# Adding the gated expert sums to the residual rows with accumulating DMAs instead of VectorE

## The reference, cut to what matters

```python
# routed_experts: y_assign holds each row's two expert outputs, wts their weights
y = einsum('tkd,tk->td', y_assign.reshape(T, 2, D), wts)
# run_trunk, after the experts
x = x + g2 * y                       # g2: a per-channel gate, one for the prompt, one for the sample
return rms_norm(x, norm_final)       # x * rsqrt(mean(x*x) + 1e-6) * norm_final
```

## Time and profile before

| What | Value |
|---|---|
| median of three runs | 1786.58 us |
| span of the profiled execution, first to last instruction | 1783.6 us |
| median less that span | 3.0 us |
| VectorE busy over the whole span | 71% |
| TensorE busy over the whole span | 91% |
| last expert matmul | 1726 us |
| first tail matmul | 1741.16 us |
| last VectorE instruction ends | 1778.8 us |

### The profile page before, as it was taken

One profiled execution on the slowest core, in us unless ns is written; L12 is line 12 of the kernel. 1 busy time (PEld: TensorE's weight loads), 2 busy tenths in 40 slices (PEclk: granted clock), 3 DMA queues, 4 the chain that ended last, 5 costly groups with the idle time before them and its releaser, 6 DMA issues. The chain is left out here.

```text
span 1783.6 us, 26138 instructions
## 1 busy us (share of the span) xinstructions
PE 1620.1 (91%) x10760; PEld 1416.7 (79%) x10760; DVE 1268.5 (71%) x1509; ACT 935.0 (52%) x1138; POOL 294.1 (16%) x187
## 2 busy tenths in 40 slices
PE   3679999999989999999798998499999999999956
PEld 2459988998889999999698786388888888888842
DVE  2535266627767768585765536799999999999947
ACT  2624233623443636353201211488888989898932
POOL 0110000200110102010200000124443232323130
PEclk9789999999999999999899998699999999999987
DMA  9822101210120202113343533699999999999966
GB/s 349 326 51 61 50 25 37 95 44 25 37 90 25 88 27 63 40 51 124 122 150 136 183 126 140 246 348 380 385 387 391 390 380 387 377 389 389 383 217 242
DMA packets 129219, 345.98 MB, mean 194 GB/s; under 512 B 16034, under 2 KB 71946, under 8 KB 103436
## 3 DMA queue, kind: packets, MB, share of 16 engines
q1 hardware_dynamic: 113180, 312.37, 48.1%
q0 software_dynamic: 9824, 17.88, 2.7%
q10 hardware_dynamic: 6096, 14.04, 2.1%
HBM read 316.15 MB, written 43.83 MB: 202 GB/s over the span
## 5 line engine op out<-in xcount | busy, mean ns | idle before, releaser
L140 PE MATMUL x_psum_proj<-h_hi,x_w_hi 128*128 128x364 f32 (+1 forms) x1120 | 381.1, 340 | 9.3 <-ACT x_x L796 6.1
L141 PE MATMUL x_psum_proj<-h_lo,x_w_hi 128*128 128x364 f32 (+1 forms) x1120 | 369.8, 330 | 0.0
L142 PE MATMUL x_psum_proj<-h_hi,x_w_lo 128*128 128x364 f32 (+1 forms) x1120 | 369.4, 330 | 0.0
L140 PEld LDWEIGHTS x_psum_proj<-h_hi,x_w_hi 128*128 128x128 f32 x1120 | 211.9, 189 | 17.6 <-ACT x_x L796 7.3
L141 PEld LDWEIGHTS x_psum_proj<-h_lo,x_w_hi 128*128 128x128 f32 x1120 | 212.1, 189 | 2.4
L142 PEld LDWEIGHTS x_psum_proj<-h_hi,x_w_lo 128*128 128x128 f32 x1120 | 212.0, 189 | 0.0
L572 POOL CAST x_w_hi<-x_w 128x1024 fp32r<-128x1024 f32 x44 | 73.5, 1671 | 636.4 <-PE x_psum_proj L142 633.8
L1978 POOL DMA_INDIRECT scratch_y<-e_y,all_tbl x32 | 73.6, 2300 | 374.9 <-ACT e_y L2091 362.1
L1186 DVE TENSOR_REDUCE x_sc<-x_diag 64x64 f32<-64x448 f32 x136 | 126.6, 931 | 1.1
L1211 DVE TENSOR_TENSOR x_w_lo<-x_w,x_w_hi 128x1024 fp32r<-128x1024 f32 x52 | 64.3, 1237 | 72.5 <-POOL x_w_hi L572 72.3
L140 PE MATMUL e_psum_g<-e_g_hi,e_x_hi 128*128 128x512 f32 x256 | 104.9, 410 | 9.6 <-DVE e_x_lo L2215 9.6
(11 more groups left out here) (350 smaller groups left out, 3775.0 us busy)
## 6 DMA issues: line engine op xcount, KB each, us to landing
mg_ring_hi<-in_w_e_gate SPq DMA_DIRECT2D x34, 1024.0 KB, 9.7
mg_ring_lo<-in_w_e_down SPq DMA_DIRECT2D x34, 1024.0 KB, 8.5
mg_ring_hi<-in_w_e_up SPq DMA_DIRECT2D x32, 1024.0 KB, 8.2
mg_ring_lo<-in_w_e_up SPq DMA_DIRECT2D x32, 1024.0 KB, 8.2
mg_ring_lo<-in_w_e_gate SPq DMA_DIRECT2D x30, 1024.0 KB, 9.3
mg_ring_hi<-in_w_e_down SPq DMA_DIRECT2D x30, 1024.0 KB, 7.9
c_w<-in_w_ada SPq DMA_DIRECT2D x12, 2048.0 KB, 15.0
x_w<-in_w_in SPq DMA_DIRECT2D x44, 512.0 KB, 3.9
```

Of the source, the lines that this page charges most:

```text
L140: nc.tensor.matmul(out, lhs[0], rhs[0], start=start, stop=False)
L141: nc.tensor.matmul(out, lhs[0], rhs[1], start=False, stop=False)
L142: return nc.tensor.matmul(out, lhs[1], rhs[0], start=False, stop=stop)
```

## The change

`x3_ready` becomes nine semaphores, one per tile. VectorE's `mixed(t)` ends with the gated product in `ys[t, 1]`. GpSimd, once it has raised `combined` and seen that the residual rows are loaded, waits for each `y_gated` in turn and issues one DMA from chip memory to chip memory that adds `ys[t, 1]` to `x3[t]`. ScalarE's `square(t)` waits for that DMA's semaphore.

```diff
+        x3_ready = [s.sem(f"x3_ready{t}") for t in range(NTT)]
...
             pool.sem_inc(combined, 1)
+            pool.wait_ge(x2_in, 16 * 3)
+            for t in range(NTT):
+                n = TILES[t][1]
+                pool.wait_ge(y_gated, t + 1)
+                pool.dma_start(x3[t][0:n], ys[0:n, t, 1, :], accum_op=ALU.add).then_inc(x3_ready[t], 16)
...
             def square(t):
                 n = TILES[t][1]
-                act.wait_ge(x3_ready, t + 1)
+                act.wait_ge(x3_ready[t], 16)
...
                     V.tensor_tensor(yt, sums[t % 2][0:n, :], g2[0:n, g, :], ALU.mult).then_inc(y_gated, 1)
-                dve.wait_ge(y_gated, t + 1)
-                V.tensor_tensor(x3[t][0:n], x3[t][0:n], yt, ALU.add).then_inc(x3_ready, 1)
-
             def normed(i):
```

More of the change, by code:

```diff
@@ L1904, in experts @@
         rows_in, x2_in, y_in = s.sem("rows_in"), s.sem("x2_in"), [s.sem(f"y_in{t}") for t in range(NTT)]
-        y_scaled, y_summed, y_gated, x3_ready, sumsq, rstd_act, rstd_dve, out_ready, out_done = (
-            s.sem("y_scaled"), s.sem("y_summed"), s.sem("y_gated"), s.sem("x3_ready"), s.sem("sumsq"), s.sem("rstd_act"),
+        x3_ready = [s.sem(f"x3_ready{t}") for t in range(NTT)]
+        y_scaled, y_summed, y_gated, sumsq, rstd_act, rstd_dve, out_ready, out_done = (
+            s.sem("y_scaled"), s.sem("y_summed"), s.sem("y_gated"), s.sem("sumsq"), s.sem("rstd_act"),
             s.sem("rstd_dve"), s.sem("out_ready"), s.sem("out_done"))
```

## The result

| | before | changed |
|---|---|---|
| median, runs of one chip | 1786.89 us (4 runs, 1786.47 to 1787.41) | 1801.74 us (4 runs, 1800.95 to 1803.04) |
| ratio, 95% interval | | 1.0088 (1.0075 to 1.0101) |
| span of the profiled execution | 1783.6 us | 1801.2 us |

The change makes the kernel slower by 14.9 us by the medians; the forecast was 1801.5. The profiled execution of the changed kernel took 1803.04 us, so 1.84 lie outside its span (the 3.0 of the prediction compared two different executions). To compare tails I measure in every profile from ScalarE's first instruction of the tail (1736.14 before, 1737.35 after) to the end of VectorE's last: 42.64 us before, 58.90 after, **+16.3**. The other 1.2 us of the 17.6 between the spans had come up earlier, where nothing was changed.

The account below looks back on a forecast made before the run. VectorE was taken to bound the last 27 us; its end became 1771.4 plus three landings summing to 22.3, 1793.7, which is 14.9 later, so the median 1786.6 + 14.9 = 1801.5 us, range 1792 to 1812.

Parts of the forecast that it names:

- The new chain: Combining tail, step by step: each normed group starts after a landing VectorE waits for, those of tiles 2, 5 and 7.
- 1771.4 + sum: VectorE's end in the tail: 1771.4 us plus L0, L1 and L2, against 1778.78 before; forecast 1793.7.
- L0: Tile 2, from end of gate multiplication to its accumulation's landing, beside the loads: 10.3 us, ends 5 and 13.
- the crowded scatter: GpSimd's scatter while weights stream: 10.3 us, read as about one packet per DMA engine in 0.8 us; used for L0.
- even sharing: Rival: GpSimd's queue gets every second turn beside the loads; landings sum to 16, +8.6 us, 1795; chance 0.19 with otherwise short DMAs.
- L1: Tile 5, from end of gate multiplication to landing, partly behind tile 4's accumulation: 6.3 us, ends 3.8 and 10.3.
- L2: Tile 7, from end of gate multiplication to landing, behind group 1's last outputs: 5.7 us, ends 3.8 and 10.3.
- the quiet case: One accumulation landing while nothing else moves: 2.6 us fixed plus 2.5 us for reading both operands, 5.1 us.
- R: From a group's last landing to the start of its normed on VectorE: 1.85 us, including 0.1 for the hand-over.
- The accumulations slow the loads ... nothing: Loads of ys slowed at most by the accumulations' volume; TensorE wants tile 8 some 10 us after arrival: no cost.
- The slow addition: Rival: each accumulation takes about a crowded scatter's time even alone; L1 and L2 9 to 10, sum 32, 1811; chance 0.15.
- The other side: Rival: chip-to-chip transfers land far sooner, 1.7 us each, sum 5.1, -2.3 us, 1784.3; decides below 7.4; chance 0.06.

Follow-up runs that it names:

- e5: Changed kernel with each accumulating DMA cut to the first 128 of 1024 columns, all waits and packets kept: 1794.19 us against 1786.22 before, ratio 1.0050.
- e3: Changed kernel with SyncE's loads of tiles 5 to 8 held until tile 2's accumulation has landed: 1803.91 us against 1786.01 before, ratio 1.0095.
- e9: Changed kernel with only tiles 2, 5 and 7 added by DMA, the other six by VectorE: 1799.52 us against 1785.56 before, ratio 1.0079.
- e1: Kernel before, VectorE's additions kept, plus nine accumulating DMAs into unread memory that only GpSimd awaits, at its end: 1799.23 us against 1786.01, ratio 1.0071.
- e4: Changed kernel with VectorE's order alone changed: gate multiplications of tiles 0 to 6 before normed(0), 7 and 8 before normed(1): 1794.81 us, ratio 1.0043.
- e2: Changed kernel with its nine DMAs copying instead of accumulating, so the residual is left out: 1794.78 us against 1786.01 before, ratio 1.0043.
- e8: Kernel before with tiles 3 and 6 added by GpSimd's own tensor_tensor, without a DMA: 1788.71 us against 1786.22 before, ratio 1.0017.

## Why the prediction was right

By its own steps:
- **The new chain.** Right in every link: `normed(0)`, `normed(1)` and `normed(2)` each start on a landing. VectorE's waits before them, 8.7, 1.8 and 6.3 us by the forecast, were 11.3, 1.8 and 5.5. The formula 1771.4 + sum, with the measured sum of 24.3 and the 1.2 us by which this execution reached the tail later, gives 1796.9; VectorE ended at 1796.25.
- **L0**, 10.3 forecast, was 13.0, inside the range but not by the mechanism that I gave. I had read the crowded scatter as one packet per engine in 0.8 us. The DMA view of the kernel before has no packet of GpSimd's queue from 1502.5 to 1508.5 us, behind a scatter issued at 1502.34; the packets of this scatter and of the gather after it, 18 per engine, all pass in the next 8 us, 0.44 us each. The view from 1508.5 to 1516.5:

```profile
q1 hardware_dynamic: 379, 2.76, 84.6%
q0 software_dynamic: 288, 0.52, 16.9%
```

  In the changed kernel it is the same. Tile 0's accumulation is issued at 1741.77, and from 1742 to 1746 us the view has SyncE's queue alone (first line); from 1748 to 1762 the two queues have equally many packets (the other two):

```profile
q1 hardware_dynamic: 201, 1.52, 103.4%
...
q0 software_dynamic: 392, 1.46, 52.1%
q1 hardware_dynamic: 394, 2.92, 51.8%
```

  So there are two parts: a wait of over 4 us until the queue's first packet, whose cause no run shows, and then even sharing, packet against packet. An accumulation's eight packets per engine take 2.83 us alone; with a packet of 8 KB between each two (0.30 us by the rival's own figure) that makes 5.2, and ScalarE's squares of tiles 0, 1 and 2 follow each other at 4.96 and 5.06 us. Tile 2 stood behind the other two, which gives the 13.0. In e5, with almost no bytes, 8.7 us are left, in e3, without loads, 5.7.
- **L1**, 6.3, was 6.4; **L2**, 5.7, was 4.9: its overlap with the outputs was nothing. Alone an accumulation takes 4.8 to 4.9 us (e9), so the 5.1 for the quiet case, built on two reads, was close.
- **R** was 1.77 us (1.85 forecast). Tile 6 at the lower clock took 6.0 (6.3), hidden as said. GpSimd's issue took 0.88.
- **"The accumulations slow the loads ... nothing"** was right for the changed kernel and wrong as a rule. Counted only as transfers beside the chain, their 24 us of all DMA engines seemed free. e1 shows them to cost 13 us by themselves, and e4 points to them as a cap on what a better order can win. In the changed kernel it did not come on top of the waits. The traffic without the waits costs 13 us (e1), the waits with an eighth of the bytes 8 (e5), and the changed kernel 14.9, less than the two together: they overlap.
- **The rivals.** Even sharing is what the queues did beside the loads; only its sum of 16 us was wrong, against 24.3. It priced an accumulation's packet at 0.15 us, by its bytes, where 2.83 us for eight is 0.35; it left out the wait before the first packet; and it counted too little for tiles 0 and 1. The sign that I gave for it, a landing of tile 2 before 1754, was therefore no test of it. The slow addition is half true, twice a copy, which the sum had; its 9 to 10 us for L1 and L2 did not come. The other side would have needed a sum under 7.4.

The 1801.5 against 1801.74 is closer than its parts, and that is luck: L0, from a misread row, came out 2.7 us long, L2 0.8 short, and the profile's +16.3 us of tail stands beside +14.9 by medians, in executions that differ by up to 2 us.

## What to carry to other kernels

Before handing an operation from a busy engine to a DMA, find the consumer that waits for it in program order. A step of 1.2 us became a landing of 5 to 13 us; in this kernel it is free only where the result is wanted some 7 us later (tiles 3 and 6), and one misplaced tile costs more than two good ones gain. Beside another full queue, count the wait for the first packet, the DMAs ahead in the same queue, and one packet of the other queue for each of its own. A landing time read from a crowded row holds all three, and they don't scale alike. Then add up the DMA engines' time over the stage, an accumulation as two copies; if the sum is longer than the stage, no order can hide it.

## What was not expected of the hardware

- Beside SyncE's loads GpSimd's queue moved no packet for some 4 us after an issue (changed kernel 4.2 at least, e5 3.9); in e9, with no load in flight, the DMA issued at 1766.52 had its first packets before 1768. The cause is not shown.
- Then the two queues took turns packet for packet, 392 against 394 in 14 us, so that an accumulation of 512 KB took 5.0 us in place of 2.5 (changed kernel, e3).
- An accumulating DMA within the chip's memory takes 2.83 us of all 16 engines per 512 KB, a copy 1.43 (changed kernel, e2).
- GpSimd's addition of 128 x 1024 takes 2.35 us and holds up VectorE's smallest step with two inputs for 2.2 to 2.3 us (e8).
